# Two transformer stacks in one kernel: the 31-tap convolution's stacked operands all through memory on SyncE's queue, and the forgetting attention as a one-place loop

## The reference, cut to what matters

```python
# "band": 12 heads of 64, and 4 memory heads
s = einsum('bqhd,bkhd->bhqk', qc, kc) * scale + bias ; p = softmax(s) ; out = p @ v
# "swa" mixer: convolution beside windowed attention, joined before one output product
a = u * sigmoid(gate)
y = depthwise_conv(a, w, 31 taps, causal) + b
yf = (y - mean(y)) * rsqrt(var(y) + EPS) * ln_g + ln_b ; a_out = silu(yf)
h = concatenate([a_out, windowed_attention(q, k, v)]) @ w_out
# "fox": forgetting attention, 16 heads of 64
sc = q @ k.T / sqrt(64) + c_t - c_s      # c = cumsum(log_sigmoid(zf + b_f))
h = (softmax(causal(sc)) @ v) @ w_out
```

## Time and profile before

| | before |
|---|---|
| median of 3 runs | 1598.29 us |
| the profiled execution | 1599.74 us, its span 1598.0 us |
| PE busy in the span | 1587.4 us (99%) |
| DVE, ACT, POOL busy | 1092.2, 919.5, 56.2 us |
| DMA | 287.67 MB, mean 180 GB/s |
| granted TensorE clock | 0.999 of full speed |
| mixer "band" | about 344 to 443 us |
| mixer "swa" with the convolution | about 829 to 915 us |
| mixer "fox" | about 1303 to 1405 us |

### The profile page before, as it was taken

The page is one execution under the profiler, slowest core; times in us unless marked ns, Lnnn a source line. Parts: engine busy times, 40 slices in busy tenths (PEclk is TensorE's granted clock), DMA queues, the critical chain, the costliest instruction groups (busy, mean ns, idle before and its releaser), DMA issues.

```text
span 1598.0 us, 23594 instructions
## 1 busy us (share of the span) xinstructions
PE 1587.4 (99%) x9256; PEld 1354.9 (85%) x9256; DVE 1092.2 (68%) x1759; ACT 919.5 (58%) x1555; POOL 56.2 (4%) x96
## 2 busy tenths in 40 slices
PE   9999999999999999999999999999999999999998
PEld 7898888889788888888887788888888889888887
DVE  5986867778677768656677466567565667775665
ACT  6766645567655546545476664447444484664544
POOL 4000000000030000000002100000000000000000
PEclk9999999999999999999999999999999999999999
DMA  8545675554355565566655555655666564356662
GB/s 299 146 146 189 217 238 192 186 174 144 118 193 190 175 199 179 188 197 189 191 159 161 143 191 186 196 185 171 210 185 188 181 200 146 119 184 199 184 189 75
DMA packets 212401, 287.67 MB, mean 180 GB/s; under 512 B 11100, under 2 KB 180382, under 8 KB 212292
## 3 DMA queue, kind: packets, MB, share of 16 engines
q1 hardware_dynamic: 208676, 280.00, 55.3%
q0 software_dynamic: 3616, 6.17, 1.4%
HBM read 284.47 MB, written 3.87 MB: 180 GB/s over the span
## 4 chain that ended last, share of the span: by engine, by line
PE 97%; DMA 1%; ACT 1%; issue 0%; SPq 0%; DVE 0%; POOL 0%; DVEq 0%; ACTq 0%
PE two L2216 91%; PE two L2293 1%; PE two L2462 1%; PE two L2475 1%; PE two L2485 1%; PE two L2870 0%; DMA vals<-u_dram 0%; PE two L2279 0%; PE two L2488 0%; DMA raw<-in_mem_w_kv 0%; PE two L2626 0%; DMA raw<-in_ffn_w_up 0%; DMA u_dram<-aux 0%; PE two L2456 0%; PE two L2844 0%
## 5 line engine op out<-in xcount | busy, mean ns | idle before, releaser
L2216 PE MATMUL two<-act_parts,w_hi 128*128 128x512 f32 (+1 forms) x2784 | 801.7, 353 | 0.0
L1488 DVE TENSOR_TENSOR w_lo<-raw,w_hi 128x1024 fp32r<-128x1024 f32 (+1 forms) x520 | 613.1, 1221 | 105.8 <-ACT w_hi L870 105.6
L2216 PE MATMUL two<-act_parts,w_lo 128*128 128x256 f32 x2256 | 635.0, 281 | 0.0
L2216 PEld LDWEIGHTS two<-act_parts,w_hi 128*128 128x128 f32 x2784 | 487.0, 188 | 81.1 <-issue 5.3
L870 ACT CAST w_hi<-raw 128x1024 fp32r<-128x1024 f32 (+1 forms) x522 | 516.6, 1046 | 5.5 <-DMA raw<-in_ffn_w_up 5.0
L2216 PEld LDWEIGHTS two<-act_parts,w_lo 128*128 128x128 f32 x2256 | 425.5, 189 | 2.1
L2216 PE MATMUL two<-w_hi,act_parts 128*128 128x512 f32 (+2 forms) x832 | 248.6, 378 | 1.5 <-ACT w_hi L870 1.2
L999 ACT COPY p_sb<-two 128x512 f32<-128x512 f32 x108 | 62.4, 578 | 247.1 <-PE two L2216 247.1
L2216 PE MATMUL two<-w_hi,hid_even 128*128 128x512 f32 x576 | 187.8, 393 | 0.0
L2216 PEld LDWEIGHTS two<-w_hi,act_parts 128*128 128x128 f32 x832 | 150.2, 188 | 33.4 <-issue 3.6
L1616 DVE TENSOR_TENSOR pt_sb<-two,p_sb 128x512 f32<-128x512 f32 x54 | 37.3, 691 | 198.4 <-ACT p_sb L999 198.4
(11 more groups left out here) (318 smaller groups left out, 1198.8 us busy)
## 6 DMA issues: line engine op xcount, KB each, us to landing
raw<-in_ffn_w_up SPq DMA_DIRECT2D x160, 512.0 KB, 3.9
raw<-in_ffn_w_down SPq DMA_DIRECT2D x132, 512.0 KB, 3.5
raw<-in_ffn_w_gate SPq DMA_DIRECT2D x80, 512.0 KB, 3.7
raw<-in_a_w_in SPq DMA_DIRECT2D x24, 512.0 KB, 4.3
raw<-in_fox_w_in SPq DMA_DIRECT2D x20, 512.0 KB, 3.8
raw<-in_ffn_w_up SPq DMA_DIRECT2D x32, 256.0 KB, 3.5
raw<-in_w_kv SPq DMA_DIRECT2D x12, 512.0 KB, 3.8
raw<-in_a_w_out SPq DMA_DIRECT2D x8, 512.0 KB, 3.8
```

Source lines behind the costliest of these rows:

```text
L1488: nc.vector.tensor_tensor(w_lo[:, r, 0:n], raw[:, r, 0:n], w_hi[:, r, 0:n], ALU.subtract).then_inc(lo_done, 1)
L2216: return nc.tensor.matmul(dst, a, w, start=start, stop=stop, skip_group_check=True)
```

## The change

**Convolution.** Chunk 0 goes through memory like the others: `stack` and `copy_stacked` are gone, `turn_u(0)` and a copy on DVE are new. The writes and reads of all four chunks are issued by SP instead of POOL, in two groups (`stack_two`): chunks 0 and 1 ahead of output slot 288, chunks 2 and 3 ahead of slot 292. Each group first waits for and writes both chunks, then waits for both writes and issues eight reads. On TensorE all four convolutions stand in one place ahead of the output product, where before `swa_out(0, ...)` stood between chunk 1 and chunk 2; `mean(3)` and `variance()` now stand behind some of the output product.

**Forgetting attention.** One function issues V(n-2), T(n-1), S(n) together, after every second half of a projection part, and then between chunks of the output product.

**Band attention.** S(3) moves up beside S(2), V(2) beside V(3), V(6) beside V(7); ACT rounds slot 139 after `pt_copy(7)` and not before `o_hi(6)`.

```diff
-            def stack(i):
...
-                            ins = nc.tensor.matmul(bank[2 + g][GRP * r:GRP * r + GRP, lo:hi], tk[:, b, at:at + GRP], moving,
-                                                   start=True, stop=True, skip_group_check=True)
-                    ins.then_inc(x_full, 1)
             def conv(c, q0=0, q1=QUADS):
-                if c:
-                    pe.wait_ge(stacked_in[c], 64)
-                else:
-                    pe.wait_ge(x_act, 2)
-                    pe.wait_ge(x_dve, 2)
+                pe.wait_ge(stacked_in[c], 64)
...
+            def stack_two(c):
+                if c == 0:
+                    sp.wait_ge(pad_out, 16 * CCH)
+                for i in (c, c + 1):
+                    sp.wait_ge(u_taken[i], 1)
+                    sp.dma_start(u_dram[i * P:(i + 1) * P, UPAD:UPAD + SEQ], cv[:, i, :]).then_inc(u_out[i], 16)
+                for i in (c, c + 1):
+                    sp.wait_ge(u_out[i], 16)
+                    for g in range(4):
+                        sp.dma_start(stacked(i, g), ...).then_inc(stacked_in[i], 16)
+            out_rows("swa", ab_w_out_2[0], {6: lambda: stack_two(0)})
+            ffn(3, ..., early={2: lambda: stack_two(2)})
...
-            project("GU1", 0, {3: [T0], 6: [T1, turn_u(1), V0]})
-            stack(0)
+            project("GU1", 0, {3: [T0], 6: [turn_u(0), turn_u(1), T1, V0]})
             scores("swa", 2)
             values("swa", 1)
-            stack(1)
-            project("GU1", 1, {3: [lambda: scores("swa", 3)]})
+            project("GU1", 1)
+            scores("swa", 3)
             conv(0, 0, QUADS // 2)
             turns("swa", 2)
             turn_u(2)
             turn_u(3)
             conv(0, QUADS // 2)
-            conv(1)
+            conv(1, 0, QUADS // 2)
             values("swa", 2)
+            conv(1, QUADS // 2)
             turns("swa", 3)
             mean(0)
+            conv(2)
+            values("swa", 3)
             mean(1)
-            values("swa", 3)
-            pe.wait_ge(u_taken[2], 1)
-            pe.wait_ge(u_taken[3], 1)
+            conv(3)
+            mean(2)
             swa_out(0, 1, 0)
             pe.wait_ge(h_olo, PAIR0["swa"] + 4)
             swa_out(0, 0, 0)
-            conv(2)
-            conv(3)
-            mean(2)
             mean(3)
+            swa_out(1, 0)
+            swa_out(1, 1)
+            out_chunk("swa", swa_ready, 2, 0, (0,))
+            variance()
...
+            def fox_stages(n):
+                if n >= 2:
+                    values("fox", n - 2)
+                if n >= 1:
+                    turns("fox", n - 1)
+                if n < 8:
+                    fox_scores(n)
             for m in range(1, 4):
                 fox_part(m, 0, 0)
-                if m > 1:
-                    values("fox", 2 * m - 3)
-                fox_scores(2 * m - 2)
+                fox_stages(2 * m - 2)
                 fox_part(m, 0, 1)
-                fox_scores(2 * m - 1)
                 fox_part(m, 1, 0)
-                turns("fox", 2 * m - 2)
+                fox_stages(2 * m - 1)
                 fox_part(m, 1, 1)
-                if m < 3:
-                    turns("fox", 2 * m - 1)
-                    values("fox", 2 * m - 2)
...
+            fox_out(0, 0); fox_stages(6); fox_out(1, 0); fox_out(0, 1); fox_out(1, 1); fox_out(2, 0)
+            fox_stages(7); fox_out(2, 1); fox_out(3, 0); fox_out(3, 1); fox_out(4, 0); fox_stages(8)
```

More of the change, by code:

```diff
@@ L1325, in _ @@
             exps("band", 7)
-            splits(139)
-            o_hi("band", 6)
             pt_copy("band", 7)
             splits(140)
+            o_hi("band", 6)
             o_hi("band", 7)
@@ L2109, in _ @@
             take_u(1, 0)
-            copy_stacked(0, 1)
             splits(284)
-            scores("swa", 3)
             probs("swa", 2)
@@ L2186, in _ @@
             take_pair(0, 1)
-            for m in range(4):
-                t = fox_slots(m, 0)
-                if m:
-                    o_lo("fox", 2 * m - 2)
-                splits(t + 8)
-                scores("fox", 2 * m)
-                if m:
-                    o_lo("fox", 2 * m - 1)
-                if m < 3:
-                    take_pair(m + 1, 0)
-                probs("fox", 2 * m)
-                scores("fox", 2 * m + 1)
-                splits(t + 9)
-                probs("fox", 2 * m + 1)
-                splits(t + (11 if m == 3 else 10))
-                if m < 3:
-                    take_pair(m + 1, 1)
+            for n in range(6):
+                t = fox_slots(0, 0) + 2 * n
+                splits(t + 7)
+                if n >= 2:
+                    o_lo("fox", n - 2)
+                scores("fox", n)
+                splits(t + 8)
+                take_pair(n // 2 + 1, n % 2)
+                probs("fox", n)
+            o_lo("fox", 4)
+            scores("fox", 6)
+            splits(450)
+            probs("fox", 6)
+            splits(451)
+            o_lo("fox", 5)
+            scores("fox", 7)
+            splits(452)
+            probs("fox", 7)
+            splits(454)
             o_lo("fox", 6)
-            splits(454)
+            splits(455)
             o_lo("fox", 7)
@@ L2934, in _ @@
             swa_out(0, 0, 0)
-            conv(2)
-            conv(3)
-            mean(2)
             mean(3)
-            for b in range(NTB):
-                swa_out(1, b)
-            variance()
-            for i in range(2, 4):
-                for b in range(NTB):
-                    swa_out(i, b)
+            swa_out(1, 0)
+            swa_out(1, 1)
+            out_chunk("swa", swa_ready, 2, 0, (0,))
+            variance()
+            out_chunk("swa", swa_ready, 2, 0, (1,))
+            swa_out(2, 1)
+            for b in range(NTB):
+                swa_out(3, b)
             for b in range(NTB):
@@ L3012, in _ @@
             fox_out(1, 1)
-            fox_scores(7)
-            for b in range(NTB):
-                fox_out(2, b)
-            turns("fox", 6)
-            for b in range(NTB):
-                fox_out(3, b)
-            turns("fox", 7)
-            values("fox", 6)
+            fox_out(2, 0)
+            fox_stages(7)
+            fox_out(2, 1)
+            fox_out(3, 0)
+            fox_out(3, 1)
             fox_out(4, 0)
+            fox_stages(8)
+            fox_out(4, 1)
             values("fox", 7)
@@ L3024, in _ @@
             out_end("fox", pair_ready("fox", 0), 0)
-            for i in range(4, NCH - 2):
-                fox_out(i, 1)
+            fox_out(5, 1)
             out_end("fox", pair_ready("fox", 0), 1)
```

167 lines of the change are left out of this document (68 added, 99 removed).

## The result

The changed kernel takes 1618.1 us (median of 4 runs, 1616.3 to 1618.8) against 1598.5 beside it: a ratio of 1.0121, interval 1.0105 to 1.0136. The forecast was 1594.0, with 1598.6 as the upper end of its range. The change makes the kernel 1.2% slower, some 20 us.

What follows compares the result with a forecast made beforehand. TensorE, busy nearly throughout the touched mixers, was taken as the bound. Swa -3.0, band -1.7 and forgetting attention +0.4 sum to -4.3 us: 1594.0 us from a median of 1598.29, range 1591.8 to 1598.6.

Steps and rivals of the forecast that it cites:

- The three places: Band attention: S(3) beside S(2), V(2) beside V(3), V(6) beside V(7) gain 0.6, 0.5 and 0.6 us.
- the same without the 0.14: Band, V(6) beside V(7): gains like V(2) beside V(3), minus the 0.14 us for T behind V; -0.6 with a wait.
- part 1, what goes: Swa convolution: stacks, old wait, a mean's wait and a return removed, `turn_u(0)` added; -4.0 us without a new wait.
- a stall of 1.1: Third convolution: due at 878.1, operand there at 879.2 if the fourth read lands in 2.0 us.
- -4.0 + 1.0: Swa mixer: removed work and waits plus the stall taken for the third convolution, -3.0 us in all.
- the new wait: Third convolution waits for its stacked operand's last read through SP; taken as 1.0 us, up to 5.3.
- Rival A: Swa: reads land on SP's queue as late as from POOL; stall 5.3 us instead of 1.0, 1598.3 us; 20%.
- nothing else is on SP's row between slot 291 and slot 292: Swa, second group: a reason to price its reads like SP's own small transfers, giving a 1.0 us stall.
- The first two have far more room: First two convolutions: operands come in good time; writes can go at 858, first convolution due at 869.
- rival C: Forgetting loop: softmax longer than its cover; at 8.5 us +10.8, total 1604.4 us; 6%.
- C's rule: Forgetting loop: beyond 6.7 us of softmax chain, each us costs one us in each of six stages.
- softmax of 4.7 to 5.3: Forgetting attention: softmax time in us set against T(5)'s 5.2 us of matmul cover, within a range of 0 to +1.5.

Runs made afterwards that it cites:

- run with reads cut by shifts: Changed kernel with each chunk's four reads split by shift, 32 channels outermost, and chunks 2 and 3 placed elsewhere: 1604.42 us, ratio 1.0033.
- mended loop: Changed kernel with reads split by shift, `probs` ahead of the splits and `o_lo(5)` ahead of `splits(451)` on DVE: 1596.05 us, ratio 0.9982.

## Why the prediction was wrong

**Band: right, a little small.** Forecast -1.7, measured -2.3 and -2.0 alone. The three places give -0.7, -0.6 and -0.9 in the overlaid traces, forecast -0.6, -0.5 and -0.6. The third was mis-sized: I took it "the same without the 0.14", but in the kernel before V(6) stands directly ahead of T(7) too, so that the 0.14 belongs in it. The 0.15 left isn't placed.

**Swa, part 1, what goes: right.** With the reads spread, the mixer comes to -3.0 (run with reads cut by shifts), with a wait of 0.68 in the place and of the kind forecast ("a stall of 1.1"). Three more runs have these reads on SyncE's queue, with waits of 0.15, 0.86 and 0.92 and a mixer of -3.5, -2.8 and -2.7; less the wait each of the four gives -3.6 or -3.7, against the forecast -4.0. That the sum -4.0 + 1.0 was met so exactly is luck, and so is the stall: the write landed in 1.90 us where I took 3.88, and the last read in 4.52 where I took 2.0.

**Swa, the new wait: wrong, and this is the step that failed first.** The prediction priced the reads' landing by other transfers: 2.0 us for 64 KB on SP's queue, 4.3 and 6.26 from POOL, and held 5.3 us for the worst stall. On SP's queue reads of this shape keep a fourth of the DMA engines busy, as the share of 0.27 to 0.29 and its rise to 0.98 by a change of nested steps show. Reads of the same shape from POOL had a share of 0.86 in the kernel before, so they were no bound for it, and no row gave a price for this shape on SyncE's queue. The engines' number on which one read lands can't be seen in a trace here; that it is four of sixteen, one for each step of the outermost dimension, fits the share on SyncE's queue and isn't shown; from POOL the same steps did not hold the share down. Rival A was the right worry with the wrong mechanism: while the reads ran alone, what is shared by all issuers was not the limit; this shape on this queue was.

**Swa, "nothing else is on SP's row between slot 291 and slot 292": the second failure.** True of the row of issues, and beside the point. What stands ahead of a write in a queue is all that was issued and has not yet landed: eight reads, two output slots and four transfers of 256 KB. The write took 10.62 us for that and not 3.88. With the reads spread and the same row of issues it took 1.90, so this failure hangs on the first: there, what stood ahead was moved in time. "The first two have far more room" fell by the same: the second convolution waited 4.1 us.

**Swa, what a wait costs beyond itself: left out.** Against -4.0 the mixer is 15.2 us worse. Two waits are 4.10 + 6.09 = 10.2. The first half of the second convolution takes 1.7 more (3.64 against 1.93) and the third convolution 2.2 more (5.80 against 3.59 of the fourth), both at a clock of 0.50; that leaves 1.1, of which V and the means behind the waits are a part. This says where the time lies and not what a cure of the clock would give back: with both waits filled by matmuls the mixer stayed at +11.1.

**Fox: rival C, which I gave 6%.** I took +0.4 for an order without waits. The mended loop shows that a stage was rightly counted: it takes 2.83 us, the sum of the prediction's pieces (V 0.80, T 0.80, S 1.03) and one return of 0.20. The mixer as a whole is +1.1 with it and not +0.4; a wait of 0.2 for `o_lo(5)` is in that, and the other 0.5 isn't placed. What failed is the softmax chain against its cover of 6.7 us. I had listed its members for C, "DVE now has `o_lo` and two `splits` in between", and then argued against it with the chain of the kernel before, where no split stood there for even n, and no `take_pair` for odd n. Adding the members' durations gives it: DVE 1.4, ACT 1.87 + 0.94, DVE 1.22 + 0.60 + 0.10 + 1.02 and some gaps are 7.3 us, from the end of S to T. In the stages inside the loop that is 0.6 a stage, as C's rule has it; C's 8.5 us was too long, and the range's "softmax of 4.7 to 5.3" was too short. The larger part came at the ends: T(0) waits 1.42 us and T(5) up to 2.1, with less cover, and S(7) 0.7 for `o_lo(5)`.

**The two rules of the Trainium skill.** By its page "DMA: Bandwidth & Descriptors", section "Issuing engines are not separate DMA queues", another issuing engine saves only issue time, which was to give a stall of 5.3. With the change's reads POOL and SyncE differ (swa +5.8 and +11.2), so it does not hold for them; with the reads spread they differ by 1.8 in the traces and not in the times, so there it nearly does. By its page "TensorEngine Tiling (Array Packing)", section "Tiling Modes", a change of mode drains TensorE. The traces agree in kind, at the 0.14 and 0.20 that the rows gave.

## What to carry to other kernels

When a transfer moves to another queue, price it from a transfer with the same nested steps on that queue, or not at all: give the unknown its own upper end. Count everything issued and not landed ahead of it, and not just what the list has next to it. When an engine's list is rewritten, add up every member that now stands between two ends of a chain, other work too, and compare it with the cover; work that isn't urgent (here a slot's rest) belongs behind the link that somebody waits for. Read a transfer's share and rate only in a stretch in which nothing else moves.

## What the runs showed of the hardware

- The order of a DMA's nested steps, with the bytes, the row size and the number of DMAs as they were, moved the DMA share while the reads ran alone from 0.27 to 0.98 (91 to 229 GB/s) on SyncE's queue, and the kernel by 13 us (1.0116 to 1.0033).
- Reads of the slower shape, alone on POOL's queue, had a share of 0.86 and 1.05, at 172 and 177 GB/s.
- Behind such reads on SyncE's queue the issue itself was slow, 1.42 us instead of 0.5, and output slots landed in 11.9 us (5.7 with the reads spread, 4.4 before).
- After idle waits of 4.10 and 6.09 us on TensorE the granted clock was 0.50 for some microseconds; with the wait filled by matmuls up to 0.5 us it stayed 1.00.
- V, T and S in a row cost the sum of their pieces and one return: 2.83 us, and 2.68 with T first (runs with `probs` ahead of the splits).
